# The z gate and merged blocks one to three of both layers go to channels through DRAM and VectorE's 32x32 transposes

## What is computed

```python
# layer 1
u   = silu(layernorm(causal_depthwise_conv(glu(glu_in)) + b_dw)) * silu(z_b)
y_b = u @ w_br_b
y_a = (rmsnorm(o_a, g_dn_out) * silu(z_a)) @ w_br_a
mixed = (sigmoid(gate_a) * y_a + sigmoid(gate_b) * y_b) @ w_out
x = x + rmsnorm(mixed, g_post)
# layer 2
merged = sigmoid(g_mla) * y_mla + sigmoid(g_conv) * y_conv
x = x + rmsnorm(merged @ w_out_2, post_norm_g)
```

## Time and profile before

| | us |
|---|---|
| median of 3 runs | 2460.87 |
| lowest, highest | 2460.4, 2461.86 |
| the profiled execution, its own time | 2461.2 |
| its span in the profile | 2459.7 |
| TensorE busy | 2414.0 (98%) |
| VectorE busy | 1605.4 (65%) |
| ScalarE busy | 1152.7 (47%) |
| mean granted TensorE clock | 0.996 |

### The profile page before, as it was taken

The page is one execution under the profiler, slowest core; times in us unless marked ns, Lnnn a source line. Parts: engine busy times, 40 slices in busy tenths (PEclk is TensorE's granted clock), DMA queues, the critical chain, the costliest instruction groups (busy, mean ns, idle before and its releaser), DMA issues.

```text
span 2459.7 us, 34106 instructions
## 1 busy us (share of the span) xinstructions
PE 2414.0 (98%) x13363; PEld 1983.8 (81%) x13363; DVE 1605.4 (65%) x2157; ACT 1152.7 (47%) x1497; POOL 165.5 (7%) x291
## 2 busy tenths in 40 slices
PE   7999999998999999999999999999999999999998
PEld 6878878787878787878888788888888888888886
DVE  5799999777676766655556664746566544555554
ACT  5444444465454545343455564544444444443443
POOL 3000000002010202010000000000000000000000
PEclk9999999999999999999999999999999999999999
DMA  7566666556343545567655565666665766685563
GB/s 230 193 205 207 206 192 216 171 184 201 121 163 121 166 134 178 200 209 281 207 183 193 167 201 184 224 208 223 197 223 188 248 198 196 199 280 188 188 223 120
DMA packets 230443, 480.59 MB, mean 195 GB/s; under 512 B 13177, under 2 KB 14050, under 8 KB 229154
## 3 DMA queue, kind: packets, MB, share of 16 engines
q1 hardware_dynamic: 214082, 418.57, 51.9%
q0 software_dynamic: 16224, 60.09, 7.2%
HBM read 451.34 MB, written 27.28 MB: 195 GB/s over the span
## 4 chain that ended last, share of the span: by engine, by line
PE 58%; DVE 1%; DMA 1%; ACT 1%; POOL 0%; issue 0%; DVEq 0%; ACTq 0%; POOLq 0%
PE acc L2371 53%; PE aux L2418 1%; PE aux L2547 1%; PE acc L2391 0%; DVE w_lo L1493 0%; PE aux L2846 0%; DMA delta_branch_spill<-ol 0%; DMA r1l<-delta_branch_spill 0%; DVE thm L2338 0%; PE aux L2851 0%; PE aux L2404 0%; PE aux L2857 0%; ACT w_hi L850 0%; PE aux L2865 0%; PE aux L2866 0%
## 5 line engine op out<-in xcount | busy, mean ns | idle before, releaser
L1493 DVE TENSOR_TENSOR w_lo<-raw,w_hi 128x1024 fp32r<-128x1024 f32 x790 | 964.9, 1224 | 781.3 <-ACT w_hi L850 770.8
L850 ACT CAST w_hi<-raw 128x1024 fp32r<-128x1024 f32 x790 | 826.3, 1049 | 1145.1 <-PE acc L2371 1134.3
L2371 PE MATMUL acc<-w_hi,r1h 128*128 128x512 f32 x1904 | 755.1, 397 | 9.3 <-DVE w_lo L1493 4.8
L2371 PE MATMUL acc<-w_lo,r1h 128*128 128x512 f32 x1904 | 740.4, 389 | 0.0
L2371 PE MATMUL acc<-w_hi,r1l 128*128 128x512 f32 x1904 | 740.1, 389 | 0.0
L2371 PE MATMUL acc<-w_hi,r2h 128*128 128x512 f32 x1208 | 473.3, 392 | 0.1
L2371 PE MATMUL acc<-w_hi,r2l 128*128 128x512 f32 x1208 | 470.3, 389 | 0.0
L2371 PE MATMUL acc<-w_lo,r2h 128*128 128x512 f32 x1208 | 470.2, 389 | 0.0
L2371 PEld LDWEIGHTS acc<-w_hi,r1h 128*128 128x128 f32 x1904 | 358.4, 188 | 91.3 <-DVE w_lo L1493 6.8
L2371 PEld LDWEIGHTS acc<-w_hi,r1l 128*128 128x128 f32 x1904 | 358.5, 188 | 75.3
L2371 PEld LDWEIGHTS acc<-w_lo,r1h 128*128 128x128 f32 x1904 | 358.9, 188 | 68.8
(11 more groups left out here) (476 smaller groups left out, 1501.1 us busy)
## 6 DMA issues: line engine op xcount, KB each, us to landing
raw<-in_w_in SPq DMA_DIRECT2D x264, 1024.0 KB, 5.0
raw<-in_w_out SPq DMA_DIRECT2D x32, 1024.0 KB, 5.0
raw<-in_w_br_b SPq DMA_DIRECT2D x16, 1024.0 KB, 5.2
raw<-in_w_br_a SPq DMA_DIRECT2D x16, 1024.0 KB, 7.0
raw<-in_w_ple_gate SPq DMA_DIRECT2D x16, 1024.0 KB, 5.0
raw<-in_w_o_mla SPq DMA_DIRECT2D x16, 1024.0 KB, 5.0
raw<-in_w_o_conv SPq DMA_DIRECT2D x16, 1024.0 KB, 4.9
raw<-in_w_q_b SPq DMA_DIRECT2D x8, 1024.0 KB, 5.0
```

Of the source, the lines that this page charges most:

```text
L850: nc.scalar.copy(w_hi[:, h % HL, 0:n], raw[:, k % RAW, x * HALF:x * HALF + n]).then_inc(hi_ready, 1)
L1493: V.tensor_tensor(w_lo[:, h % HL, 0:n], raw[:, k % RAW, x * HALF:x * HALF + n], w_hi[:, h % HL, 0:n].bitcast(F32), ALU.subtract).then_inc( ...
L2371: ins = T.matmul(acc[:, s, x, 0:n], a[:, kt0 + k, xs_], w[:, h % HL, at], start=start and k == 0 and m == 0, stop=stop and k == kts - 1 an ...
```

## The change

Three matters at once. First, the turns: z gate blocks 0 to 3, merged blocks 0 to 2 of layer 1 and of layer 2 no longer go through `channels_first`; GpSimd turns them through DRAM (landing in `u`, `us` and `oin`, which are free then), VectorE transposes in 32x32 blocks at step 6 or 7 of the next block (steps 15, 23, 31 and 11 for the z gate, 14, 22 and 30 in YA and YC), and ScalarE and VectorE make high and low part from SBUF. ScalarE's `szT_copy` goes; its factor 0.25 moves into the multiplication of `LN_GATE`. Second, `decay_rows(0)` moves forward in GpSimd's queue to just behind `ln_out(0)`, and the multiplication with the decay rows moves in VectorE's `delta` from step 1 to step 14. Third, in QKVZ `i` = 0 the transposes of `k` move from step 28 to step 27.

```diff
-OWN_FIRST = ((8, 9, 10, (11, 15), 16, 19), (16, 20, 21, (22, 24), 25, 28), (24, 25, 26, (27, 29), 30, 31))
+OWN_FIRST = ((8, 9, 10, (11, 15), 16, 19), (16, 20, 21, (22, 24), 25, 27), (24, 25, 26, (27, 29), 30, 31))
...
+            def turn_gate(j):
+                pool.wait_ge(acc_free[j % 2], freed(PH["ZB"], j))
+                if j:
+                    pool.wait_ge(sem("szT_ready"), j)
+                turn(sz0[:], u[:].rearrange("p t n -> p (t n)"), j + 1)
+            pool.wait_ge(sem("uT_tr"), NJ)
+            for j in range(NJ - 1):
+                turn_gate(j)
             rsqrt(var[:], var[:], 1.0 / PARTS, sem("square_ready"), SQ_LN)
+            turn_gate(NJ - 1)
...
             ln_out(0)
+            pool.wait_ge(sem("egc_out"), 16 * (P // 32))
+            decay_rows(0)
             ln_out(1)
...
             columns_k(0, True)
             pool.wait_ge(sem("uT_out"), 32 * NJ)
-            pool.wait_ge(sem("egc_out"), 16 * (P // 32))
-            decay_rows(0)
...
-            for j in range(2, NJ):
-                pool.wait_ge(sem("m_ready"), OP_M + j - 1)
-                load_gate(0, j, j % 2)
+            for j in range(NJ - 1):
+                pool.wait_ge(sem("m_ready"), OP_M + j + 1)
+                if j + 2 < NJ:
+                    load_gate(0, j + 2, j % 2)
+                turn(mtmp, us_land, TURNS_YA + j + 1)
...
+            for j in range(NJ - 1):
+                pool.wait_ge(sem("m_ready"), OP_Y + j + 1)
+                turn(thz[:], oin[:, 0].rearrange("p t n -> p (t n)"), TURNS_YC + j + 1)
...
# ScalarE
-            def szT_copy(j):
-                act.wait_ge(sem("zT_tr"), j + 1)
-                for q in range(2):
-                    sig(A(szT[...], X[:, 2 + q]..., ACT.Copy, scale=0.25), "szT_ready", 2 * j + q + 1)
...
+            def turned_hi(dst, tile, j, base, turn):
+                act.wait_ge(sem("m_turned"), turn)
+                for q in range(2):
+                    sig(A(dst[:, CT * j + 2 * q:CT * j + 2 * q + 2], tile[:, 2 * q:2 * q + 2], ACT.Copy, scale=0.5), "m_hi", 2 * (base + j) + q + 1)
...
-                if at_block(hl, 2) is not None:
-                    merged_hi(r2h, at_block(hl, 2), OP_M)
+                if at_block(hl, 6) is not None:
+                    turned_hi(r2h, mtmpT, at_block(hl, 6), OP_M, at_block(hl, 6) + 1)
...
# VectorE
+            def gate_turned(j):
+                sig(turned(szT[:, j * CT:(j + 1) * CT], u[:].rearrange("p t n -> p (t n)"), j + 1), "szT_ready", j + 1)
...
+                if at_block(hl, 7) is not None:
+                    gate_turned(at_block(hl, 7))
...
-                if hl == 1:
+                if hl == 14:
                     dve.wait_ge(sem("egc_landed"), dv(32, 32))
                     sig(V.tensor_tensor(flat(qdT), flat(qT), flat(egc_rep), ALU.mult), "qdT_ready", dv(1, 1))
...
+                if hl == 11:
+                    gate_turned(NJ - 1)
...
-                    sig(V.tensor_tensor(q4(y, q), q4(y, q), q4(szT, q), ALU.mult), "ln_out", q + 1)
+                    sig(V.scalar_tensor_tensor(q4(y, q), q4(szT, q), 0.25, q4(y, q), ALU.mult, ALU.mult), "ln_out", q + 1)
...
-                if at_block(hl, 2) is not None:
-                    merged_lo(r2h, r2l, at_block(hl, 2), OP_M)
+                if at_block(hl, 6) is not None:
+                    j = at_block(hl, 6)
+                    sig(turned(mtmpT, us_land, TURNS_YA + j + 1), "m_turned", j + 1)
+                if at_block(hl, 7) is not None:
+                    turned_lo(r2h, r2l, mtmpT, at_block(hl, 7), OP_M)
...
# TensorE
-                if at_block(hl, 2) is not None:
-                    z_transposed(at_block(hl, 2))
...
-                if hl == 2:
-                    z_transposed(NJ - 1)
...
-                if at_block(hl, 1) is not None:
-                    merged_tr(mtmp, at_block(hl, 1), OP_M)
...
-                if at_block(hl, 1) is not None:
-                    merged_tr(thz, at_block(hl, 1), OP_Y)
```

More of the change, by code:

```diff
@@ L56 @@
 TURN_LANDED = 16 * (P // TURN)
+TURNS_YA = NJ
+TURNS_FC = TURNS_YA + NJ - 1
+TURNS_YC = TURNS_FC + 2 * NJ
+MTR_YA, MTR_ATTN, MTR_Y = 0, 1, 1 + NJ
 SHORT = 4
@@ L423, in build_layer @@
         mtmp = kbe[:].rearrange("p t h d -> p t (h d)")
+        mtmpT = kbe[:].rearrange("p t h d -> p (t h d)").rearrange("p (a n) -> p a n", a=CT)
+        thzT = thz[:].rearrange("p t n -> p (t n)").rearrange("p (a n) -> p a n", a=CT)
+        us_land = us[:].rearrange("p t h d -> p (t h d)")
         acc = ctx.enter_context(nc.psum_tensor("acc", [P, 2, TT, NB], F32))
@@ L811, in _ @@
                 pool.wait_ge(acc_free[1], freed(PH["FC"], 5, i))
-                turn(cg[:], turn_land, 2 * i + 1)
+                turn(cg[:], turn_land, 2 * i + 1 + TURNS_FC)
                 pool.wait_ge(acc_free[1], freed(PH["FC"], 7, i))
-                turn(zs[:], turn_land, 2 * i + 2)
+                turn(zs[:], turn_land, 2 * i + 2 + TURNS_FC)
                 pool.wait_ge(sem("c_lo"), i + 1)
@@ L1238, in _ @@
                 if hl == 2:
[L1239 removed]
+                    merged_hi(r2h, NJ - 1, OP_M, MTR_YA + 1)
                 if at_block(hl, 0) is not None:
@@ L1464, in _ @@
                 if hl == 2:
-                    merged_hi(r1h, NJ - 1, OP_Y)
+                    merged_hi(r1h, NJ - 1, OP_Y, MTR_Y + 1)
                 if at_block(hl, 0) is not None:
@@ L1971, in merged_lo, with turned_lo @@
                                                hi[:, kt].bitcast(F32), ALU.mult, ALU.subtract), "m_lo", 2 * (base + j) + q + 1)
+            def turned_lo(hi, lo, tile, j, base):
+                for q in range(2):
+                    dve.wait_ge(sem("m_hi"), 2 * (base + j) + q + 1)
+                    kt = slice(CT * j + 2 * q, CT * j + 2 * q + 2)
+                    sig(V.scalar_tensor_tensor(lo[:, kt], tile[:, 2 * q:2 * q + 2], 0.5,
+                                               hi[:, kt].bitcast(F32), ALU.mult, ALU.subtract), "m_lo", 2 * (base + j) + q + 1)
             ph = PH["YA"]
@@ L2306, in _ @@
                     merge2(at_block(hl, 0))
-                if at_block(hl, 2) is not None:
-                    merged_lo(r1h, r1l, at_block(hl, 2), OP_Y)
+                if at_block(hl, 6) is not None:
+                    j = at_block(hl, 6)
+                    sig(turned(thzT, oin[:, 0].rearrange("p t n -> p (t n)"), TURNS_YC + j + 1), "m_turned", NJ - 1 + j + 1)
+                if at_block(hl, 7) is not None:
+                    turned_lo(r1h, r1l, thzT, at_block(hl, 7), OP_Y)
             ph = PH["OUT"]
@@ L2929 @@
     arrays = {name: np.ascontiguousarray(inputs[name]) for name in _INS}
-    PERMUTED = [("w_in_2", C2_CIN, 4 * NJ)]
+    PERMUTED = [*[(name, 0, NJ - 1) for name in ("w_br_a", "w_br_b", "w_o_mla_2", "w_o_conv_2", "b_gate")], ("b_gate", D, NJ - 1),
+                *[("w_in", C_GATE + at, NJ - 1) for at in (0, D)], *[("w_in_2", at, NJ - 1) for at in (C2_GM, C2_GC)],
+                ("w_in", C_ZB, NJ), ("w_in_2", C2_CIN, 4 * NJ)]
     for name, first, blocks in PERMUTED:
```

24 lines of the change are left out of this document (8 added, 16 removed).

## The result

The change made the kernel slower: 2469.8 us median of 5 runs against 2460.6 of 5 runs of the kernel before beside them, ratio 1.0036 (95% interval 1.0024 to 1.0048). I had forecast 2447.8. The profiled execution has a span of 2466.4 us, where 2459.7 stood before; 6.7 us more.

A forecast was written before the change was run, and what follows sets the result against it. TensorE, holding 58% of the chain, was taken to bound the kernel. Terms -9.0 - 7.2 + 0.5 + 0.3 + 0.95 + 1.3 = -13.1 us took 2461.2 to 2448.1, as median 2447.8; range 2444 to 2454.5.

The forecast's parts named there:

- Transposes, -9.0 us: ZB, QKVZ 0, YA, YC: 80 transposes in ten groups leave TensorE, saving 0.90 us a group, 9.0 us.
- Decay rows, -7.2 us: QKVZ 1 alone: earlier decay rows and a later product remove TensorE's wait for `uinv` and its slow clock, saving 7.2 us.
- VectorE's new work, +3.05 us: Added VectorE work partly delays TensorE: 0.5, 0.3 and 0.95 us in QKVZ 0, 1.3 over four `delta` stages.
- the 0.5 and 0.3 of the forecast: QKVZ 0: z gate turns on VectorE cost 0.5 us at the start (step 31) and 0.3 at step 11.
- The waits that come with a turn: YA, YC, ZB: DRAM round trips fit the available time, and later loads on GpSimd's queue land in time; cost 0.
- one of its own signs of being wrong: The forecast would be wrong if TensorE waited for low parts in YA or YC; two other signs were named.
- The lead of 5.6 us: YA, YC: TensorE's weights are ready 5.6 us ahead, said to cover VectorE's and ScalarE's turn work and late turns.
- The room of 13.8 us for a trip: YA: from the merged block's end to VectorE's transpose at step 14, 13.8 us; a trip within that is free.
- The round trip: YA: write to DRAM and read back, sized from FC at 11.3 us, 11.8 with a gate load, say 12.1.
- rival E: YA, YC: late turns stall TensorE six times, from some 21.5 us on; twice 12.1 us costs 29, giving 2477; chance 0.05.
- `p`, "10 us are left": End of YA: `p`, issued 7.5 us after the third merged block, has 10 us left to land before MIX.
- The clock: QKVZ 1: TensorE's granted clock falls to 0.54 for some 4 us after idling; its recovery is part of the 7.2 us.

The follow-up runs named there:

- the kernel without trips: Changed kernel with the six turns of merged blocks left out of GpSimd's queue, other engines' work kept: 2451.0 us, ratio 0.9963 to the kernel before.
- the spacing: Changed kernel, fourth-block transposes two steps later, `p` and gain rows ahead of the third turn, turned blocks' roundings at separate steps: 2450.4 us, ratio 0.9962.
- the run before the spacing: Changed kernel with fourth-block transposes two steps later and `p` and the gain rows issued ahead of the third turn: 2457.1 us, ratio 0.9985.

## Why the prediction was wrong

- **Transposes, -9.0 us: right.** ZB is 2.68 us shorter for three groups, and so is YC wherever nothing is late: 0.90 for a group, as read from the starts.
- **Decay rows, -7.2 us: right**, by a run of their own. TensorE had no wait for `uinv`, and the slow clock of the earlier trace rows went with it.
- **VectorE's new work, +3.05 us: nearly right.** It was about 3.9: QKVZ 0 lost 2.0 beside the 0.9 gained, and step 14 cost 0.5 us in each of four stages (I took 0.33). `k` at step 27 cost 0.9, a wait of 0.7 and its refill (I took 0.95). With `k` at 28, QKVZ 0 is 0.06 us shorter than before, though a group of transposes is gone from it (0.9): so the rest of the turn's work costs 0.8 there, in sum the 0.5 and 0.3 of the forecast.
- **The waits that come with a turn, "Cost 0": wrong, and this is the step that failed.** It put at nothing what cost 19.4 us, and one of its own signs of being wrong came: TensorE waited for low parts in YA and YC. Four parts of it:
  1. *The lead of 5.6 us was taken as the cover for everything.* It covers weights only. TensorE's own transposes of block four have no lead: they stand one step behind the forming of the block. I counted who waits for the turned block and not who waits for what VectorE does next: `merge`, which stands in line behind the waiting transpose, is nowhere in the forecast's count. Moving the transposes two steps gave back 11 to 12 us.
  2. *The room of 13.8 us for a trip was read from a kernel without turns.* It held for the first turn of a stage (13.9 and 13.8) and for no other: 11.2 and 11.8 were left for the second, 9.5 for the third. About 2 us go with any turn, even without a trip (ready at 7.1 us, not 5.0), the rest with the lateness of the turn before.
  3. *The round trip was sized at 12.1 us from FC, and took 13.4 to 14.9 in five of six cases* (10.6 in the first of YC). Landing alone, from the last issue to the last landing, took 5.9 to 8.0 us in those five, in FC of the same trace 3.2 to 4.7. FC's turns stand 40 us or more apart. In YC a late turn went with a longer next trip; in YA the first one was long too, and why stays open.
  4. *The lead was counted twice.* ScalarE's wait in line takes 2.5 us of it even when a turn is on time (2.45 in the kernel without trips), and VectorE's wait for ScalarE follows (2.52 there, the 2.51 above). By these the 5.6 would have been used up by a lateness of about 3 us, an estimate.

  So rival E was the right one by its nature, yet it was said to decide from 21.5 us on, and with "x 6". Trips of 13.4 to 14.9 us were enough, and the cost came mostly once in a stage. Its price, 29 us for trips twice as long, was for a path that the trace doesn't show.
- **`p`, "10 us are left": wrong.** `p` was issued 7.7 us after the third merged block, close to the 7.5 of the forecast. But that block was ready 10.6 us into step 24, not 4, and `p` took 7.6 us to land (1179.91 to 1187.5), behind the third turn's reads, in a time when the DMA engines were full. TensorE was there at 1184.66, 4.8 us after the issue. The gap and the slow half behind it took 4.7 us of the profiled execution; what its mending is worth by the medians stays open (0.3 us, in runs that spread by 4 and 9).
- **The clock.** I had used it for the gain in QKVZ 1 and not for the loss. Each of the three waits was followed by 1.5 to 1.75 us of slow matmuls, 4.8 us of the 19.4.

The missing 19.4 us of YA to OUT, by halves: 1.2 + 1.2 (low parts in YA and YC), 3.1 (`p`), 1.6 (slow half behind it), 2.8 and 6.9 (block four), 1.5 and 1.7 (slow halves behind it), less 0.6 for another gap of YA that was shorter this time: 19.4. Forecast and median are 22.0 us apart, while the spans of the profiled executions miss the forecast by 19.8: the one after was 1.9 us faster than its median, the one before 0.3 slower.

## What to carry to other kernels

When an instruction is made to wait on an in-order engine, follow the queue behind it to the first thing that the bounding engine itself takes in order, and take *that* thing's slack, not the buffers' lead. Read the room for a wait with the new work in place: here the second and third turn had 2 to 4 us less of it than the first, because each turn made the next block late. Space the consumers out (each engine one step behind the last), so that none stands in line for another, and don't take a transfer's time from another stage: FC's didn't hold in YA. A later use can cost nothing: two steps for two groups of transposes gave back 11 to 12 of 19 us.

## What the runs showed of the hardware

- The last read of 128 KB of a turn landed 5.9 to 8.0 us after its issue in five of six turns of YA and YC in the changed kernel, and 3.2 to 4.7 in FC. In YC it was 3.7 to 5.3 with the spacing, in YA 6.1 to 8.2 even so. The two weight chunks beside the second read of YC landed after 7.1 and 9.3 us in the changed kernel, 6.8 and 8.9 in the run before the spacing, 5.1 and 6.3 with it.
- In the changed kernel, behind a wait of TensorE of 2.8 us seven matmuls started 0.43 us apart (MIX, below), which cost 1.5 us; behind one of 5.9 us it was eight (from 2373.18), 1.75 us. That is no fixed price. Other kernels had waits of 1.5 and 1.7 us (no trips) and 2.2 (`p`, blocks 1 and 2 turned) with no such matmul behind them, one of 6.7 with four of them (blocks 0 and 1), one of 4.2 with three (blocks 1 and 2, in MIX), and one of 4.6 with eleven (later transposes, in front of MIX). The loss doesn't follow the length of the wait.

```profile
1198.03 1.33 PE L2458 MATMUL aux<-ident,kbe 128*128 128x128 f32 x8 [2.77 <-DVE kbe L1991]
...
1199.58 0.63 PE L2411 MATMUL acc<-w_lo,r2h 128*128 128x512 f32 x1
...
1202.14 0.41 PE L2411 MATMUL acc<-w_lo,r2h 128*128 128x512 f32 x1
```
